# Masked attentions: value products of two query tiles together, key block by key block

## The chip, the cores and the metric

The kernel runs on one core of one Trainium2 chip. The metric is the device time of one execution in microseconds (us). PE is the matrix engine (TensorE; PEld its weight loads), ACT is ScalarE, DVE is VectorE, POOL is GpSimd, SP is SyncE, which issues most transfers.

## The reference, cut to what matters

The program is a chain of transformer layers over 512 tokens of width 1024: a convolution module, a feed-forward layer, a gate, a "forgetting" attention with 16 heads of 64, another feed-forward layer and gate, and a second block with three branches, one of them a block attention with 8 heads of 64. Both attentions with heads of 64 are causal and carry a bias per key:

```
s  = einsum("bqhd,bkhd->bhqk", q_blk, k) + bias      # q_blk: 128 queries
s  = where(k_pos <= q_pos, s, NEG_BIG)
pr = softmax(s, axis=-1)
o  = einsum("bhqk,bkhd->bqhd", pr, v)
```

In the second (`moba_attention`) a query sees its own block of 256 keys and up to three earlier ones. With 512 tokens there is one earlier block, which is always selected, so it too is causal attention over all keys, with a distance bias per head. Everything is in fp32.

## The kernel before, in words

Data lie with features on the partitions and the 512 tokens along the free axis. The large matrix products are done in three passes of a faster 32-bit format (high x high, high x low, low x high; L592 to L594), with weights that come from memory through `raw` and are split by ACT (L1062) and POOL (L485). Most of the time goes into these. The attentions are between them: the first between the projections of keys and values and the output projection, the second between two branches of the second block.

`head_attention` is written once for each of PE, ACT and DVE, and called for both attentions (`fox`, 8 head pairs; `mob`, 4 head pairs), with the biases fetched by SP or made by POOL. Each engine runs its own list of instructions in the order written; semaphores tie them together. Work is cut into groups: group `i` is one head pair (`j = i // 4`, heads `hh` = 0 and 1) and one tile of 128 queries, in the order of `ROW_TILE = (0, 3, 1, 2)`. A causal tile `qb` sees `qb + 1` key blocks of 128, so that the groups of a pair have 1, 4, 2 and 3 blocks. `s = 2 * i + hh` numbers a group's heads. For a group:

- PE `S_`: scores, 64 rows deep, both heads side by side (L855), and the causal mask as a product with a triangle (L857).
- DVE `B_`: bias, minimum and row maximum (L1880), into the group's own buffer of `prob_of` (in T and U).
- ACT `E_`: exponential with the row sum (L1327).
- DVE `R_`: reciprocal (L1887) and weighting (L1891).
- PE `T_`: transpositions, one per head and key block, with the identity (L866), into bank 2 + `hh` of `ms`. It waits for the weighting, and for the copy that last emptied this bank (`pt_copied`).
- ACT `C_`: the copy of a head's turned weights to `probT` (L1335). There are four such buffers of 512 columns: `U[:, 1]`, `acc_sq` and the two halves of `sqb`; buffer `s % 4` is free when the value products two groups back are done (`pv_done`).
- PE `V_`: value products, per key block and head a product of 64 value columns with 128 turned weights, added up over key blocks in bank 2 + `j % 2` of `gp` (L877).
- After a pair's last group: ACT `H_` (L1339) copies the output's high half, DVE `L_` (in the helper at L1532) makes its low half.

The order on PE is set by hand: iteration `i` does `S_(i)`, `T_(i - 3)`, `V_(i - 4)`. On ACT it is, for each of the two heads, the copy `C_` of group `i - 3` and the exponential `E_` of group `i`, and in every fourth iteration `H_`. On DVE it is `B_` of group `i` and `R_` of group `i - 1`, and in every fourth iteration `L_`. Of an fp32 product the trace has two records for each matmul, except for transpositions, which have one.

`wgx` is a gate weight of a later branch; it is cleared by POOL and filled by transfers after the first attention, and last read before the second.

Of the kernel before, what the change touches and what calls it, by code (L numbers as in the profile page):

```python
# [18 lines left out]
F32 = mybir.dt.float32  # L19
# [3 lines left out]
ACT = mybir.ActivationFunctionType  # L23
AX = mybir.AxisListType

P = 128
S = 512
D = 1024
KB = D // P
QB = S // P  # L30
# [15 lines left out]
ROW_TILE = (0, 3, 1, 2)  # L46
# [66 lines left out]
def build(nc, hbm, out):  # L113
# [6 lines left out]
    def phase(slabs=0, blks=0, rows=8, src=0, tiles=4, wide=False, **more):  # L120

        at = {"slab": led.take("slab", slabs), "blk": led.take("blk", blks)}
        of = rows if isinstance(rows, list) else [-1 if wide else rows] * slabs
        slab_at.extend(src + s // 2 for s in range(0, slabs))
        b = at["blk"]
        for s, r in enumerate(of):  # L130
            if wide:
                b += 4 * (s % 4 == 2)
                freed_at.append(Wide(led.take("wide", s % 4) + 1) if s % 4 < 2 else b)
                continue
            b += 8 // r if r else tiles * (1 - s % 2)
            freed_at.append(b)
        rows_of.extend(of)
        at.update({k: led.take(k, n) for k, n in more.items()})
        return at
# [22 lines left out]
    gq = phase(slabs=8, blks=8, src=53)  # L162
    gk = phase(slabs=8, blks=8, src=57)
    gv = phase(slabs=8, blks=8, wide=True, src=61)
    fox = phase(split=8, step=64, weighted=64, pt=64, pv=32)
    wo = phase(slabs=8, src=65, blks=8, split=8, sq=8, acc=7, norm=1, stat=1)
    plan_ffn(1)
    fin = phase(split=8)
# [8 lines left out]
    gkm = phase(slabs=4, blks=4, src=120)  # L177
    gvm = phase(slabs=4, blks=4, wide=True, src=122)
    br[0] = phase(slabs=12, blks=16, rows=branch_rows, src=124, sg=8, gm=8)
    mob = phase(split=4, step=32, weighted=32, pt=32, pv=16)  # L180
    br[1] = phase(slabs=12, blks=16, rows=branch_rows, src=130, sg=8, gm=8)
    mrg = phase(split=8)
    wout = phase(slabs=8, src=136, blks=8, split=8, sq=8, acc=7, norm=1, stat=1)
# [4 lines left out]
    with ExitStack() as ctx:  # L188
        def sb(name, shape, dt=F32, where=ctx):
            return where.enter_context(nc.sbuf_tensor(name, shape, dt))  # L190
# [15 lines left out]
        inv_d = sb("inv_d", [P, P])  # L206
        ident, identb, tri = sb("ident", [P, P]), sb("identb", [P, P], BF16), sb("tri", [P, P], BF16)
        T = sb("T", [P, 4, S])
        U = sb("U", [P, 2, S])
        acc_sq, sqb = sb("acc_sq", [P, S]), sb("sqb", [P, 2, S])  # L210
        rstd, var = sb("rstd", [P, S]), sb("var", [P, S])
        mkv = sb("mkv", [P, 4 * S])
        mk = mkv[:, 0:4 * MEM].rearrange("p (c s) -> p c s", c=4)
# [22 lines left out]
        with ExitStack() as lc:  # L236
            merged = sb("merged", [P, KB, S], F32, lc)
            with ExitStack() as c1:
                qx = sb("qx", [P, 4, S], F32, c1)
            with ExitStack() as c2:  # L240
                xap = sb("xap", [P, 4, S + 3], F32, c2)
                ga = sb("ga", [P, 4, S], F32, c2)
                xc = sb("xc", [P, 4, S], F32, c2)
                wga, wgx = sb("wga", [P, 4, P], F32, c2), sb("wgx", [P, 4, P], F32, c2)
            with ExitStack() as c3:
                qm, vm = sb("qm", [P, 4, S], F32, c3), sb("vm", [P, QB, HALF], F32, c3)
                mbias = sb("mbias", [P, 4, S], F32, c3)
                dist = sb("dist", [P, S], F32, c3)
        with ExitStack() as ld:
# [2 lines left out]
        big = u_pad[:, :, TAPS - 1:]  # L252
        bigs, proj_sb = (big, big1), kT
        prob, probT = T, (U[:, 1, :], acc_sq, sqb[:, 0, :], sqb[:, 1, :])
        prob_of = (T[:, 2, 3 * P:], T[:, 3, 3 * P:], U[:, 0, 0:2 * P], U[:, 0, 2 * P:],
                   T[:, 2, 0:3 * P], T[:, 3, 0:3 * P], T[:, 0, :], T[:, 1, :])
        token_half = (slice(0, S // 2), slice(S // 2, S))
# [4 lines left out]
        mcol = sb("mcol", [P, 2])  # L262
        mem_sq = mkv[:, :].rearrange("p (k s) -> p k s", k=KB)
        SP_OPS = 9 + len(ATANH)
        def whole_at(i):

            return TAPS - POOL_TAPS[i] - PE_TAPS[i]
# [15 lines left out]
        def conv_end(i, s=1):  # L283
# [3 lines left out]
        gp = ctx.enter_context(nc.psum_tensor("gp", [P, 4, S], F32))  # L287
        ms = ctx.enter_context(nc.psum_tensor("ms", [P, 4, S], F32))
# [37 lines left out]
        scored, biased, exped, transposed, pt_copied, pv_done, sum_inv = (  # L326
            sem("scored"), sem("biased"), sem("exped"), sem("transposed"), sem("pt_copied"), sem("pv_done"),
            sem("sum_inv"))
# [7 lines left out]
        step_open, weighted = sem("step_open"), sem("weighted")  # L336
# [247 lines left out]
        def _(pe):  # L584
# [252 lines left out]
            def head_attention(at, n, queries, keys, values, before):  # L837

                t0, N = at["step"], 4 * n

                def S_(i):
                    j, qb = i // 4, ROW_TILE[i % 4]
                    w, bank = (qb + 1) * P, (ms, gp)[i % 2]
                    if i == 1:
                        for c in range(2):
                            wait_evac(pe, before, c)  # L850
                    if i >= 2:
                        pe.wait_ge(biased, t0 + 2 * i - 2)
                    for hh in range(2):
                        r = slice(64 * hh, 64 * hh + 64)
                        pe.matmul(bank[:, hh, 0:w], queries[r, j, qb * P:qb * P + P], keys[r, j, 0:w], start=True, stop=False)  # L855
                    for hh in range(2):
                        pe.matmul(bank[:, hh, qb * P:w], identb[:], tri[:], start=False, stop=True).then_inc(scored, 1)  # L857

                def T_(i):
                    for hh in range(2):  # L860
                        s = 2 * i + hh
                        pe.wait_ge(weighted, at["weighted"] + s + 1)
                        if i:
                            pe.wait_ge(pt_copied, at["pt"] + s - 1)
                        for kb in range(ROW_TILE[i % 4] + 1):
                            m = pe.transpose(ms[:, 2 + hh, kb * P:kb * P + P], prob_of[2 * ROW_TILE[i % 4] + hh][:, kb * P:kb * P + P], ident[:])  # L866
                        m.then_inc(transposed, 1)

                def V_(i):
                    j, qb = i // 4, ROW_TILE[i % 4]  # L870
                    pe.wait_ge(pt_copied, at["pt"] + 2 * i + 2)
                    if i % 4 == 0 and j >= 2:
                        pe.wait_ge(lo_done, at["split"] + j - 1)
                    for kb in range(qb + 1):
                        for hh in range(2):
                            c = j * P + 64 * hh
                            m = pe.matmul(gp[64 * hh:64 * hh + 64, 2 + j % 2, qb * P:qb * P + P], values[:, kb, c:c + 64],  # L877
                                          probT[(2 * i + hh) % 4][:, kb * P:kb * P + P], start=(kb == 0), stop=(kb == qb),
                                          skip_group_check=True)
                    m.then_inc(pv_done, 1)  # L880

                for i in range(N + 4):
                    if i < N:
                        S_(i)
                    if 3 <= i < N + 3:
                        T_(i - 3)
                    if i >= 4:
                        V_(i - 4)

            head_attention(fox, 8, qT, kT, v_s, Pos(gv["blk"] + 4))  # L890
            gemm(wo, A, ready=fox["split"])
# [155 lines left out]
        def _(act):  # L1047
# [46 lines left out]
            for s, ready in enumerate((half_ready, raw_ready[0])):  # L1094
                src, at = part(Pos(s))
# [224 lines left out]
            def head_attention(at, X, k0, n):  # L1320
                t0, N = at["step"], 4 * n

                def E_(s):
                    w = (ROW_TILE[s // 2 % 4] + 1) * P
                    act.wait_ge(biased, t0 + s + 1)
                    p = prob_of[2 * ROW_TILE[s // 2 % 4] + s % 2][:, 0:w]
                    act.activation(p, p, ACT.Exp, scale=-1.0, bias=nmax[:, s % 8:s % 8 + 1], accum_out=rsum[:, s % 8:s % 8 + 1]  # L1327
                                   ).then_inc(exped, 1)

                def C_(s):  # L1330
                    w = (ROW_TILE[s // 2 % 4] + 1) * P
                    act.wait_ge(transposed, t0 + s + 1)
                    if s >= 4:
                        act.wait_ge(pv_done, at["pv"] + s // 2 - 1)
                    act.activation(probT[s % 4][:, 0:w], ms[:, 2 + s % 2, 0:w], ACT.Copy).then_inc(pt_copied, 1)  # L1335

                def H_(j):
                    act.wait_ge(pv_done, at["pv"] + 4 * (j + 1))
                    act.activation(X[0][:, k0 + j], gp[:, 2 + j % 2], ACT.Copy).then_inc(hi_done, 1)  # L1339

                for i in range(N + 3):
                    for s in (2 * i, 2 * i + 1):
                        if i >= 3:
                            C_(s - 6)
                        if i < N:
                            E_(s)
                    if i >= 8 and i % 4 == 0:
                        H_(i // 4 - 2)
                H_(n - 1)
# [942 lines left out]
```

## Time and profile before

| | |
|---|---|
| median of 3 runs | 2135.89 us (2135.56 to 2137.75) |
| profiled execution | 2135.93 us, its span 2134.1 us |
| PE busy | 2090.2 us (98%), granted clock 0.995 of full |
| ACT, DVE busy | 800.4 us (38%), 1012.6 us (47%) |
| the first attention on PE | 769.9 to 846.5 us |
| the second attention on PE | 1577.7 to 1619.5 us |

A record's length on PE is a modelled latency, and matmuls overlap: their pace is the distance of their starts. In a timeline, equal neighbours are merged ("x16"): the first number is the start of the first, the second the time from there to the end of the last. What stands in brackets is the engine's idle time before it and the releaser that the view infers from semaphores.

### The profile page before, as it was taken

How to read it: one execution, taken by the hardware profiler on the slowest of the kernel's cores; microseconds unless marked ns; L12 is line 12 of the kernel's file. 1: busy time of each engine (PE TensorE's matmuls, PEld its weight loads, DVE VectorE, ACT ScalarE, POOL GpSimd, SP SyncE). 2: the span in 40 equal slices, each digit the busy share in tenths (PEclk: the TensorE clock that was granted, in tenths of full speed). 3: DMA queues.
4: the chain of work that ended last, by engine and by line, in shares of the span. 5: the costliest groups of instructions: out<-in, count | busy, mean ns of one | idle time of the engine just before them, and what ended most of it. 6: DMA issues, size and time to landing. Idle time of an engine off the chain costs nothing.

```text
span 2134.1 us, 26391 instructions
## 1 busy us (share of the span) xinstructions
PE 2090.2 (98%) x9842; PEld 1697.7 (80%) x9842; DVE 1012.6 (47%) x1584; ACT 800.4 (38%) x1235; POOL 937.9 (44%) x437
## 2 busy tenths in 40 slices
PE   8998999999999999999999999999999999999998
PEld 6776888888888866888888887878867888888887
DVE  7996623122364556442131355573454456254463
ACT  6755422222353157322222355352244343222222
POOL 5984544444444420354444442444442444444442
PEclk9998999999999999999999999999999999999999
DMA  5332322222222221232222221322211222222221
GB/s 192 117 131 79 138 99 99 98 98 98 99 80 100 99 90 63 88 118 99 98 98 98 98 81 60 104 79 99 99 60 60 91 91 97 106 90 99 98 98 60
DMA packets 34523, 205.31 MB, mean 96 GB/s; under 512 B 4592, under 2 KB 6768, under 8 KB 11520
## 3 DMA queue, kind: packets, MB, share of 16 engines
q1 hardware_dynamic: 34144, 199.87, 26.8%
q10 hardware_dynamic: 288, 4.19, 0.5%
q8 instruction: 60, 0.98, 0.2%
q14 instruction: 31, 0.25, 0.0%
HBM read 197.73 MB, written 6.32 MB: 96 GB/s over the span
## 4 chain that ended last, share of the span: by engine, by line
PE 59%; issue 23%; POOL 10%; DVE 6%; ACT 1%; DMA 0%; POOLq 0%; DVEq 0%; ACTq 0%
PE gp L592 18%; PE gp L594 18%; PE gp L593 18%; POOL w_lo L485 9%; DVE ms L1535 4%; POOL pool_sum L508 1%; PE gp L640 0%; PE gp L639 0%; PE gp L638 0%; PE ms L729 0%; PE gp L937 0%; PE gp L877 0%; DMA raw<-w_hbm 0%; PE ms L740 0%; DVE T L1532 0%
## 5 line engine op out<-in xcount | busy, mean ns | idle before, releaser
L485 POOL TENSOR_TENSOR w_lo<-raw,w_hi 128x1024 fp32r<-128x1024 f32 x350 | 848.5, 2427 | 1102.0 <-ACT w_hi L1062 1080.3
L592 PE MATMUL gp<-a_hi,w_hi 128*128 128x512 f32 (+1 forms) x1456 | 568.2, 390 | 9.7 <-DVE a_lo L1535 8.8
L594 PE MATMUL gp<-a_hi,w_lo 128*128 128x512 f32 (+1 forms) x1456 | 563.9, 387 | 0.0
L593 PE MATMUL gp<-a_lo,w_hi 128*128 128x512 f32 (+1 forms) x1456 | 563.8, 387 | 0.0
L1062 ACT ACTIVATE w_hi<-raw 128x1024 fp32r<-128x1024 f32 x349 | 365.6, 1051 | 507.9 <-PE gp L594 436.9
L593 PE MATMUL gp<-b_lo,w_hi 128*128 128x512 f32 (+1 forms) x1216 | 470.4, 387 | 0.0
L592 PE MATMUL gp<-b_hi,w_hi 128*128 128x512 f32 x1184 | 463.8, 392 | 3.3 <-DVE b_lo L1532 3.3
L594 PE MATMUL gp<-b_hi,w_lo 128*128 128x512 f32 x1184 | 461.4, 390 | 0.0
L592 PEld LDWEIGHTS gp<-a_hi,w_hi 128*128 128x128 f32 x1456 | 273.9, 188 | 68.4 <-issue 10.5
L593 PEld LDWEIGHTS gp<-a_lo,w_hi 128*128 128x128 f32 x1456 | 274.0, 188 | 57.0 <-issue 1.4
L594 PEld LDWEIGHTS gp<-a_hi,w_lo 128*128 128x128 f32 x1456 | 273.8, 188 | 55.6
L1532 DVE TENSOR_TENSOR h<-gp,h 128x512 f32<-128x512 f32 (+1 forms) x106 | 72.2, 681 | 424.4 <-PE gp L594 424.4
L593 PEld LDWEIGHTS gp<-b_lo,w_hi 128*128 128x128 f32 x1216 | 229.0, 188 | 47.5 <-issue 1.2
L592 PEld LDWEIGHTS gp<-b_hi,w_hi 128*128 128x128 f32 x1184 | 222.8, 188 | 52.3 <-issue 5.6
L594 PEld LDWEIGHTS gp<-b_hi,w_lo 128*128 128x128 f32 x1184 | 222.6, 188 | 46.2
L1532 DVE TENSOR_TENSOR T<-gp,rstd 128x512 f32<-128x512 f32 x136 | 93.8, 691 | 309.0 <-PE gp L594 306.8
L1535 DVE SCALAR_TENSOR_TENSOR ms<-u_pad,par,ms 128x512 f32<-128x512 f32 x176 | 120.2, 757 | 0.8
L1071 ACT ACTIVATE sqb<-h 128x512 f32<-128x512 f32 x61 | 38.4, 630 | 129.7 <-DVE h L1532 116.3
L1535 DVE SCALAR_TENSOR_TENSOR T<-gpad,par,T 128x512 f32<-128x512 f32 x48 | 83.4, 1737 | 5.2 <-DVE T L2114 0.2
L508 POOL TENSOR_TENSOR pool_sum<-pool_sum,sqb 128x512 f32<-128x512 f32 x48 | 61.1, 1292 | 11.0 <-ACT sqb L1153 11.0
L1253 ACT ACTIVATE b_hi<-U 128x512 fp32r<-128x512 f32 x32 | 20.3, 634 | 121.3 <-DVE U L1535 121.3
L1253 ACT ACTIVATE a_hi<-U 128x512 fp32r<-128x512 f32 x32 | 20.3, 634 | 120.6 <-DVE U L1535 120.6
(327 smaller groups left out, 1797.2 us busy)
## 6 DMA issues: line engine op xcount, KB each, us to landing
raw<-w_hbm SPq DMA_DIRECT2D x175, 1024.0 KB, 4.8
proj_scratch<-kT ACTq DMA_DIRECT2D x2, 2048.0 KB, 6.9
fbias<-negc_scratch SPq DMA_DIRECT2D x16, 256.0 KB, 3.4
h<-x_hbm SPq DMA_DIRECT2D x8, 256.0 KB, 7.6
u_pad<-proj_scratch SPq DMA_DIRECT2D x1, 2048.0 KB, 9.8
big<-proj_scratch SPq DMA_DIRECT2D x1, 2048.0 KB, 8.8
out_hbm<-h SPq DMA_DIRECT2D x8, 256.0 KB, 2.2
raw<-w_hbm SPq DMA_DIRECT2D x2, 512.0 KB, 6.6
```

The source lines that it names most:

```text
L485: g.tensor_tensor(at(w_lo), src, f32(at(w_hi)), ALU.subtract).then_inc(w_lo_done, 1)
L508: g.tensor_tensor(pool_sum[:, s], pool_sum[:, s], sqb[:, s], ALU.add).then_inc(pool_conv, 1)
L592: pe.matmul(o, wh, xh, start=start, stop=False)
L593: pe.matmul(o, wh, xl, start=False, stop=False)
L594: return pe.matmul(o, wl, xh, start=False, stop=stop)
L1062: act.activation(at(w_hi), src, ACT.Copy).then_inc(w_hi_done, 1)
L1071: act.activation(dst, h[:, c], ACT.Square).then_inc(sq_done, 1)
L1253: act.activation(H_[0][:, k], U[:, k % 2], ACT.Copy).then_inc(hi_done, 1)
L1532: return v.tensor_tensor(o, a, b, op)
L1535: return v.scalar_tensor_tensor(o, a, s, b, op0, op1)
```

## The change

The value products of two consecutive groups of a pair (a "couple" `m`, groups `2m` and `2m + 1`: query tiles 0 and 3, or 1 and 2) are done in one batch. For each key block and head there is one product: where both tiles see the block, with 256 columns, else with 128. A batch has four or three key blocks (8 or 6 products) and comes in odd iterations: after `T_(i - 3)` comes the batch with groups `i - 5` and `i - 4`; even iterations have none, and the last batch stands behind the loop.

So that the two tiles' turned weights for one key block are neighbours, the copies go to slots of 128 columns in a tensor `turned` of 20 slots: five for each head of a couple, and two couples. Tile 3 goes to four slots in a row and tile 0 to the one ahead of it; tile 1 goes to slots 1 and 3, and tile 2 to slots 0, 2 and 4, whose blocks are transposed in the order 2, 0, 1. A copy now waits until the batch of the couple two before is done. `U`, `acc_sq` and `sqb` become parts of one tensor `scratch` with six rows, five of which are `turned`; `wgx` moves into the sixth.

```diff
-    fox = phase(split=8, step=64, weighted=64, pt=64, pv=32)
+    fox = phase(split=8, step=64, weighted=64, pt=64, pv=16)
...
-        U = sb("U", [P, 2, S])
-        acc_sq, sqb = sb("acc_sq", [P, S]), sb("sqb", [P, 2, S])
+        scratch = sb("scratch", [P, 6, S])
+        U, acc_sq, sqb = scratch[:, 0:2], scratch[:, 2], scratch[:, 3:5]
...
+        turned = scratch[:, 1:6].rearrange("p r (n c) -> p (r n) c", c=P)
...
+        turn_order = ([0], [0, 1], [2, 0, 1], [0, 1, 2, 3])
+
+        def turned_keys(m, hh, kb):
+
+            a = 10 * (m % 2) + 5 * hh
+            n, tiles = ((0, 2), (2, 1), (3, 1), (4, 1))[kb] if m % 2 == 0 else ((1, 2), (3, 2), (0, 1))[kb], (0, 3) if m % 2 == 0 else (1, 2)
+            return turned[:, a + n[0]:a + n[0] + n[1]], tiles[2 - n[1]:]
+
+        def turned_tile(m, hh, qb):
+
+            a = 10 * (m % 2) + 5 * hh
+            return turned[:, a:a + 1] if qb == 0 else turned[:, a + 1:a + 5] if qb == 3 else turned[:, a + 1:a + 4:2] if qb == 1 else turned[:, a:a + 5:2]
...
-                        for kb in range(ROW_TILE[i % 4] + 1):
-                            m = pe.transpose(ms[:, 2 + hh, kb * P:kb * P + P], prob_of[2 * ROW_TILE[i % 4] + hh][:, kb * P:kb * P + P], ident[:])
+                        qb = ROW_TILE[i % 4]
+                        for n, kb in enumerate(turn_order[qb]):
+                            m = pe.transpose(ms[:, 2 + hh, n * P:n * P + P], prob_of[2 * qb + hh][:, kb * P:kb * P + P], ident[:])
                         m.then_inc(transposed, 1)
 
-                def V_(i):
-                    j, qb = i // 4, ROW_TILE[i % 4]
-                    pe.wait_ge(pt_copied, at["pt"] + 2 * i + 2)
-                    if i % 4 == 0 and j >= 2:
+                def V_(m):
+                    j = m // 2
+                    pe.wait_ge(pt_copied, at["pt"] + 4 * m + 4)
+                    if m % 2 == 0 and j >= 2:
                         pe.wait_ge(lo_done, at["split"] + j - 1)
-                    for kb in range(qb + 1):
+                    for kb in range(QB - m % 2):
                         for hh in range(2):
                             c = j * P + 64 * hh
-                            m = pe.matmul(gp[64 * hh:64 * hh + 64, 2 + j % 2, qb * P:qb * P + P], values[:, kb, c:c + 64],
-                                          probT[(2 * i + hh) % 4][:, kb * P:kb * P + P], start=(kb == 0), stop=(kb == qb),
-                                          skip_group_check=True)
-                    m.then_inc(pv_done, 1)
-
-                for i in range(N + 4):
+                            keys_of, tiles = turned_keys(m, hh, kb)
+                            o = gp[64 * hh:64 * hh + 64, 2 + j % 2].rearrange("p (t c) -> p t c", c=P)
+                            o = o[:, tiles[0]:tiles[0] + 1] if len(tiles) == 1 else o[:, tiles[0]:tiles[1] + 1:tiles[1] - tiles[0]]
+                            mm = pe.matmul(o, values[:, kb, c:c + 64], keys_of, start=(kb == 0), stop=(kb == QB - 1 - m % 2), skip_group_check=True)
+                    mm.then_inc(pv_done, 1)
+
+                for i in range(N + 3):
                     if i < N:
                         S_(i)
-                    if 3 <= i < N + 3:
+                    if i >= 3:
                         T_(i - 3)
-                    if i >= 4:
-                        V_(i - 4)
+                    if i >= 5 and i % 2:
+                        V_((i - 5) // 2)
+                V_(N // 2 - 1)
...
                 def C_(s):
-                    w = (ROW_TILE[s // 2 % 4] + 1) * P
+                    m, qb, hh = s // 4, ROW_TILE[s // 2 % 4], s % 2
                     act.wait_ge(transposed, t0 + s + 1)
-                    if s >= 4:
-                        act.wait_ge(pv_done, at["pv"] + s // 2 - 1)
-                    act.activation(probT[s % 4][:, 0:w], ms[:, 2 + s % 2, 0:w], ACT.Copy).then_inc(pt_copied, 1)
+                    if m >= 2:
+                        act.wait_ge(pv_done, at["pv"] + m - 1)
+                    act.activation(turned_tile(m, hh, qb), ms[:, 2 + hh, 0:(qb + 1) * P].rearrange("p (r c) -> p r c", c=P), ACT.Copy
+                                   ).then_inc(pt_copied, 1)
```

The high half's wait becomes `pv_done` at 2 per pair instead of 4, and the second attention's count of batches 8 instead of 16.

## Rows read from the trace of the kernel before

**Rows 1.** The page, part 1: busy time, share of the span, instructions
```profile
PE 2090.2 (98%) x9842; PEld 1697.7 (80%) x9842; DVE 1012.6 (47%) x1584; ACT 800.4 (38%) x1235; POOL 937.9 (44%) x437
```

**Rows 2.** Windows: stretch, us, busy us of PE, PEld, DVE, ACT, POOL, clock, DMA
```profile
770.00:846.00 76.00, 72.52 (x666) 45.27 (x668) 58.22 (x232) 63.77 (x200) 2.35 (x1) 1.00 0.13 43
1582.00:1620.00 38.00, 34.54 (x320) 21.80 (x317) 28.96 (x104) 29.56 (x94) 4.17 (x4) 1.00 0.01 2
...
784.90:794.15 9.25, 9.03 (x88) 5.70 (x84) 7.25 (x30) 7.88 (x26) 0.00 (x0) 1.00 0.17 59
...
821.88:831.12 9.24, 9.02 (x88) 5.70 (x84) 7.25 (x30) 7.88 (x26) 0.00 (x0) 1.00 0.18 60
```

**Rows 3.** Timeline of PE, one head pair: start us, us, what, count, [idle before]
```profile
812.73 0.49 PE L855 MATMUL ms<-kT,qT 64*128 64x128 f32 x4
...
813.28 1.04 PE L866 MATMUL ms<-ident,T 128*128 128x128 f32 x8
814.25 0.32 PE L877 MATMUL gp<-U,v_s 128*64 128x128 f32 x1
...
814.41 0.27 PE L877 MATMUL gp<-U,v_s 128*64 128x128 f32 x1
...
814.62 1.13 PE L855 MATMUL gp<-kT,qT 64*128 64x512 f32 x4
...
816.34 1.09 PE L877 MATMUL gp<-sqb,v_s 128*64 128x128 f32 x16
817.36 0.70 PE L855 MATMUL ms<-kT,qT 64*128 64x256 f32 x4
...
818.84 0.52 PE L866 MATMUL ms<-ident,T 128*128 128x128 f32 x3 [0.23 <-DVE T L1891]
819.29 0.32 PE L877 MATMUL gp<-U,v_s 128*64 128x128 f32 x1
...
819.88 0.92 PE L855 MATMUL gp<-kT,qT 64*128 64x384 f32 x4
...
820.85 0.39 PE L866 MATMUL ms<-ident,T 128*128 128x128 f32 x2
821.17 0.88 PE L877 MATMUL gp<-sqb,v_s 128*64 128x128 f32 x12
821.97 0.49 PE L855 MATMUL ms<-kT,qT 64*128 64x128 f32 x4
```

**Rows 4.** Timeline of ACT, the same head pair
```profile
813.92 0.60 ACT L1335 ACTIVATE sqb<-ms 128x512 f32<-128x512 f32 x1
...
815.66 0.59 ACT L1339 ACTIVATE a_hi<-gp 128x512 fp32r<-128x512 f32 x1
...
817.62 0.72 ACT L1327 ACTIVATE T<-T,nmax 128x512 f32<-128x512 f32 x1 [1.00 <-DVE nmax L1880]
...
818.34 0.36 ACT L1335 ACTIVATE acc_sq<-ms 128x256 f32<-128x256 f32 x1
...
820.17 0.48 ACT L1335 ACTIVATE sqb<-ms 128x384 f32<-128x384 f32 x1
```

**Rows 5.** Timeline of DVE, the same head pair
```profile
814.30 0.75 DVE L1891 TENSOR_SCALAR T<-T,rinv 128x384 f32<-128x384 f32 x2
816.28 0.69 DVE L1532 TENSOR_TENSOR a_lo<-gp,a_hi 128x512 fp32r<-128x512 f32 x1 [1.23 <-ACT a_hi L1339]
```

**Rows 6.** Timeline of PE in the ramp of the first attention
```profile
774.37 0.39 PE L866 MATMUL ms<-ident,T 128*128 128x128 f32 x2
774.69 0.49 PE L855 MATMUL ms<-kT,qT 64*128 64x128 f32 x4
```

**Rows 7.** Timeline of PE and of ACT at the end of it
```profile
845.72 0.88 PE L877 MATMUL gp<-sqb,v_s 128*64 128x128 f32 x12
...
844.79 0.87 ACT L1335 ACTIVATE sqb<-ms 128x384 f32<-128x384 f32 x2 [1.06 <-PE ms L866]
```

**Rows 8.** One line's instructions: ns min/median/max
```profile
L1062 ACT ACTIVATE w_hi<-raw x349: 1039/1046/1065, 24.4 to 2101.5; 128x1024 fp32r<-128x1024 f32 x175
```

More of the change, by code:

```diff
@@ L179, in build @@
     br[0] = phase(slabs=12, blks=16, rows=branch_rows, src=124, sg=8, gm=8)
-    mob = phase(split=4, step=32, weighted=32, pt=32, pv=16)
+    mob = phase(split=4, step=32, weighted=32, pt=32, pv=8)
     br[1] = phase(slabs=12, blks=16, rows=branch_rows, src=130, sg=8, gm=8)
@@ L243, in build @@
                 xc = sb("xc", [P, 4, S], F32, c2)
-                wga, wgx = sb("wga", [P, 4, P], F32, c2), sb("wgx", [P, 4, P], F32, c2)
+                wga, wgx = sb("wga", [P, 4, P], F32, c2), scratch[:, 5].rearrange("p (j c) -> p j c", c=P)
             with ExitStack() as c3:
@@ L1330, in C_ @@
                 def C_(s):
-                    w = (ROW_TILE[s // 2 % 4] + 1) * P
+                    m, qb, hh = s // 4, ROW_TILE[s // 2 % 4], s % 2
                     act.wait_ge(transposed, t0 + s + 1)
-                    if s >= 4:
-                        act.wait_ge(pv_done, at["pv"] + s // 2 - 1)
-                    act.activation(probT[s % 4][:, 0:w], ms[:, 2 + s % 2, 0:w], ACT.Copy).then_inc(pt_copied, 1)
+                    if m >= 2:
+                        act.wait_ge(pv_done, at["pv"] + m - 1)
+                    act.activation(turned_tile(m, hh, qb), ms[:, 2 + hh, 0:(qb + 1) * P].rearrange("p (r c) -> p r c", c=P), ACT.Copy
+                                   ).then_inc(pt_copied, 1)
                 def H_(j):
-                    act.wait_ge(pv_done, at["pv"] + 4 * (j + 1))
+                    act.wait_ge(pv_done, at["pv"] + 2 * (j + 1))
                     act.activation(X[0][:, k0 + j], gp[:, 2 + j % 2], ACT.Copy).then_inc(hi_done, 1)
```

## The prediction

> **What bounds the kernel now.** The page comes first: the matrix engine is busy 2090.2 of 2134.1 us, and no other engine passes 48% [rows 1]. Such a share is of intervals that overlap, so I went on to the windows of the two masked attentions. There the matrix engine is still the fullest (72.5 of 76 us and 34.5 of 38 us, clock at full speed), but ScalarE is busy 84% and VectorE 77% of the first attention, where over the whole program it is 38% and 47%; one pair of heads takes 9.24 us, five times running (the first and the last are shown), of which ScalarE is busy 7.88 [rows 2]. So here the question is not "how much does the matrix engine do" but "who waits for whom", and that is read from the three engines' timelines of one head pair, 812.7 to 822.0.
>
> On the matrix engine every iteration is scores (L855), mask (L857), turning (L866), value products (L877) [rows 3]. The two heads' value products start together, on 64 columns each; a pair of records of 128 columns follows the last after 0.109 us: 16 records take (1.09-0.27)/7.5. That is 128 columns at two cycles of 2.4 GHz (0.107) and 0.002 over. Entering and leaving a batch costs more: the last transposition before 814.25 starts at 813.28+1.04-0.27=814.05, so 0.20 passes where 0.11 is the pace; the second pair follows the first after 0.16 instead of 0.11; and at the exit 0.20 passes again.
>
> There is one stall in the pair: three transpositions start at 818.84 after idling [rows 3]. The view names the weighting on VectorE, but that group's weighting was over at 814.30+0.75=815.05 [rows 5]; the instruction also waits until the bank it writes has been copied out, and that copy ran 818.34 to 818.70 on ScalarE [rows 4], 0.14 before 818.84. The copy was late because ScalarE executes in order: it stood behind the exponential of 817.62, which had idled 1.00 for VectorE's biased scores, which stood behind the low half of the previous pair's output (816.28, idle 1.23), which waited for ScalarE's high half of 815.66 [rows 4, 5]. That half comes back to back behind the copy of 813.92. This closes a ring, and the ring gives the period: copy of 813.92 to the end of the copy at 818.70, 4.78; wake-up 0.14; 818.84 to the value products at 819.29, 0.45; these to the scores at 819.88, 0.59; to 820.85, 0.97; to 821.17, 0.32; to 821.97, 0.80; scores to the next such copy (812.73 to 813.92), 1.19. Sum 9.24, the measured period [rows 2 to 4].
>
> **The change, part by part.** *Matmuls.* A head pair has 20 value products (2 heads x 10 key blocks); they become 14, since blocks shared by two query tiles run once at 256 columns. Columns stay. Streaming costs the same 0.107 per pass and block; six pair slots fewer at 0.002 each are 0.01 us.
>
> *Batches.* Four become two per pair, each of five blocks. The batch of one block (814.25 to 814.62, 0.37) and that of two (0.59) go, and their blocks come back in the next iteration's batch at 0.21 each: 0.37-0.21 and 0.59-0.43, 0.16 twice. The scores now follow a transposition directly; that succession stands in the ramp: transpositions at 774.37 (two, last start 774.48) and scores at 774.69, 0.20 again [rows 6], so the exit price stays and the entry price alone goes. Gross gain on the matrix engine 0.33 per pair, 3.9 us over 12 pairs. If nothing but the matrix engine counted, that would be the answer.
>
> The Trainium skill says two things of this place. Its page "TensorE: Matmul & The Clock Gate" (section on what happens when a matmul is issued) says that weight loads are pulled ahead of running matmuls; by it, entering a batch would be free, the gross gain only 0.01 x 12=0.1, and the first rival below 2135.8 instead of 2132.0. "TensorEngine Tiling (Array Packing)", Key Properties, says "Mode switching requires drain"; by it going from 128x128 to 128x64 costs, and the gain of 3.9 stands. The rows at 814.25 side with the second [rows 3].
>
> *The copies' wait.* ScalarE's copy waited for the value batch two groups back; now it waits for the batch two pairs of groups back, which is issued at least two iterations before the transposition. It did not wait before and doesn't now: nothing.
>
> *The copies' pattern.* For two and three blocks the destination is now in pieces of 128 elements that begin 256 apart; the source stays contiguous. No row has a scattered destination on ScalarE. Nearest: the weight copies of L1062, most of which read eight pieces of 128 and some one piece of 1024; all lie within 1039 to 1065 ns [rows 8]. I take 0; above, 0.02 per copy (the spread of these), and since three such copies lie in the ring (818.34, 820.17 and the one between them), 0.06 x 12=0.7 us; below, nothing, as the number of elements stays.
>
> *The order.* This decides. In iterations with an even number there is no value batch now; in odd ones it has five blocks. Take the pair above. Up to the copy ending at 818.70 the ring is ScalarE and VectorE alone, and scores come earlier, not later: 818.84 stays where it is. From 819.29 the scores go first: they would be done 0.59 early, and the next transpositions could start at 820.26 and 820.37. But the second of them writes the bank whose copy runs 820.17 to 820.65 [rows 4], back to back behind exponentials since 817.62, so it can't be moved by the matrix engine. Before, it met a bank just free (820.85 plus 0.11); now it waits until 820.65+0.14=820.79. And behind it stands the whole batch: 0.20 to enter, then five blocks. Four blocks take 817.36-816.34=1.02; one more is 0.22, merging gives back 0.01: 1.23. The scores come at 822.22, where they came at 821.97. The new ring: ScalarE 813.92 to 820.65, 6.73; 0.14; 0.20; 1.23; 1.19; sum 9.49, **0.25 longer** per pair. The two blocks that used to fill the copy's shadow have moved behind it. The wait of 818.84 grows too (the matrix engine arrives 0.15 earlier), which costs nothing.
>
> *Ramp and tail.* The first pair runs before the ring has closed; it can gain between nothing and 0.33, and as its second head's transposition already waits for a copy I take 0.10. At the end, the last batch but one stands ahead of the last transpositions and has five blocks instead of four (+0.21); the last one starts only when the last copies are done (844.79+0.87=845.66, batch at 845.72 [rows 7]), and the two blocks that ran in their shadow come behind (+0.43): +0.64. The output's high and low halves and the next phase's first matmuls follow as before.
>
> *Memory.* Four scratch rows become one tensor with a fifth row, lent by a gate weight that is cleared and used between the attentions; no instruction is added, no queue passed. Nothing.
>
> **The sum.** First attention, eight pairs: -0.10, five closed periods x 0.25, +0.64: 1.8. Second, four pairs, taken at the same durations since its busy shares are the same to a few per cent [rows 2]: -0.10, one period 0.25, +0.64: 0.8. Together +2.6 us. The profiled execution took 2135.93 (span 2134.1 and 1.8 around it), the median of the runs shown is 2135.89: the same. Forecast 2138.5 us, slower by 0.12%, which a measurement of this kernel (about 0.2%, 4.3 us) hardly tells from no change.
>
> **Rivals.**
> *The matrix engine's gain arrives.* If the second transposition does not meet a busy bank, 0.33 x 12=3.9 us come off: 2132.0. For it: the matrix engine is the fullest in every window, and ScalarE idles 1.00 in each pair. Against: the idle time lies inside the ring, not after it. It needs ScalarE's chain of 817.62 to 820.65 to begin some 0.4 earlier, for which nothing in the change provides.
> *The existing stall goes as well.* If moving work out of the even iterations lets the high half, the low half and with them 817.62 come earlier, up to the present wait at 818.84 goes: the idle 0.23 shown there counts from the modelled end of a record 0.27 long where the pace is 0.11, so the engine stood 0.23+0.16=0.39; x 12=4.7 more: 2127.3. Against: 815.66 is followed back to 813.92 with ScalarE never idle.
> *Slower than can be overlooked.* ScalarE's copies with a scattered destination cost more. The three on the ring each lengthen every period; at 0.08 each 0.24 x 12=2.9 us come on top, +5.5: 2141.4. It decides from 0.05 per copy (+4.4). For it: no row excludes it; ScalarE has no slack there. Against: [rows 8], for the source side.
> *The heads no longer run side by side.* If 256-column products of the two heads ran one after another, each batch would take 1.07 more, 24 x 1.07=26 us: 2164. For it: nothing; the scores run side by side up to 512 columns (1.13 for four records of 0.43).
>
> **Chances.** Forecast 0.62 (+1.0 to +4.2); full gain 0.16, half of it perhaps just past the bound; stall gone too 0.05; scattered copies 0.15; heads apart 0.02. Range 2132.5 to 2141.5: it takes in the unpriced copies above and most of the first rival below. Faster by over 0.2%: 0.13; within: 0.67; slower: 0.20.
>
> **What would show it.** In the timeline of a steady pair: no L877 between L866 and L855 in even iterations; batches of 8 and 6 pair slots, 1.2 us from first start to the scores; the single transposition's second head starting about 0.5 after the first, 0.14 behind the end of a 384-column copy; a period of 9.49; copies of 256 and 384 columns at 0.36 to 0.40 and 0.48 as now. L877 has 336 records for 480. The prediction is wrong if the period is 9.24 or less, if that transposition doesn't wait, or if the copies' durations moved.

## The result, and the profile after

The changed kernel takes **2140.62 us** (median of 13 runs, 2138.67 to 2141.48) against 2136.11 (13 runs): the ratio is 1.0019, 95% interval 1.0012 to 1.0026, so 2.6 to 5.6 us slower. The forecast was 2138.5 in a range of 2132.5 to 2141.5. It also said that a measurement would hardly tell the change from none; this interval does tell it. The profiled execution took 2141.31 with a span of 2138.5.

First the page, part 1, to be read against [rows 1]. The matrix engine (PE) has 144 records fewer (12 pairs x 12), and its busy share says nothing of the loss:

```profile
PE 2091.0 (98%) x9698; PEld 1695.6 (79%) x9698; DVE 1013.3 (47%) x1584; ACT 798.1 (37%) x1235; POOL 937.9 (44%) x437
```

Then two windows, each one head pair of the first attention, as in [rows 2]. A pair takes 9.52 us where it took 9.24, and every engine but VectorE is busy for less of it:

```profile
796.13:805.65 9.52, 8.89 (x76) 5.36 (x72) 7.36 (x30) 7.64 (x26) 0.00 (x0) 1.00 0.17 56
815.18:824.70 9.52, 8.89 (x76) 5.37 (x72) 7.36 (x30) 7.64 (x26) 0.00 (x0) 1.00 0.16 55
```

The timeline of PE for the second of these pairs answers to [rows 3]; L869 are scores, L881 transpositions, L895 value products:

```profile
815.26 0.49 PE L869 MATMUL ms<-kT,qT 64*128 64x128 f32 x4
...
815.80 1.04 PE L881 MATMUL ms<-ident,T 128*128 128x128 f32 x8
816.78 1.13 PE L869 MATMUL gp<-kT,qT 64*128 64x512 f32 x4
...
818.50 1.31 PE L895 MATMUL gp<-scratch,v_s 128*64 128x256 f32 x16
819.74 0.70 PE L869 MATMUL ms<-kT,qT 64*128 64x256 f32 x4
...
821.37 0.52 PE L881 MATMUL ms<-ident,T 128*128 128x128 f32 x3 [0.38 <-DVE T L1909]
821.82 0.92 PE L869 MATMUL gp<-kT,qT 64*128 64x384 f32 x4
...
822.79 0.28 PE L881 MATMUL ms<-ident,T 128*128 128x128 f32 x1
823.32 0.30 PE L881 MATMUL ms<-ident,T 128*128 128x128 f32 x1 [0.25 <-ACT scratch L1352]
823.55 1.30 PE L895 MATMUL gp<-scratch,v_s 128*64 128x256 f32 x12
824.78 0.49 PE L869 MATMUL ms<-kT,qT 64*128 64x128 f32 x4
```

The reader is to see the new stall: the single transposition of the second head starts 0.53 after the first (822.79, 823.32). It was 0.11 before, two records running together at 820.85 [rows 3]. Behind it stands the whole batch of five blocks. The timeline of ScalarE (ACT), against [rows 4], has what it waits for:

```profile
816.45 0.60 ACT L1352 ACTIVATE scratch<-ms 128x512 f32<-128x512 f32 x1 [0.79 <-PE ms L881]
...
820.14 0.72 ACT L1344 ACTIVATE T<-T,nmax 128x512 f32<-128x512 f32 x1 [1.09 <-DVE nmax L1898]
...
820.86 0.36 ACT L1352 ACTIVATE scratch<-ms 128x256 f32<-128x256 f32 x1
...
822.69 0.48 ACT L1352 ACTIVATE scratch<-ms 128x384 f32<-128x384 f32 x1
```

The ring of the forecast can be read off step by step: copy of 816.45 to the end of the copy at 823.17, 6.72; wake-up 0.15; transposition to batch 0.23; batch to scores 1.23; scores (815.26) to the next such copy (816.45) 1.19. Sum 9.52. ScalarE now idles 0.79 ahead of the first of these copies, which it did not before: it waits for a matrix engine that waits for it. The copies last 0.36 and 0.48 as before.

**Where the 5.4 us between the two profiled executions are.** The first scores of the first attention start at 769.90 before and 771.67 after: +1.77 before the change has done anything. The first attention, from there to the first matmul of the next stage, takes 76.62 and 78.40 (+1.78); the second 41.77 and 42.13 (+0.36). What is left of the span is +0.5, and outside the span are 1.83 and 2.81 (+1.0).

### The profile page after: what moved, and what is told of

It is laid out like the page before. It is cut to its first block, busy times and chain, and to the rows that moved or that the text cites. A ratio compares the mean times of both kernels' runs of the same rounds, so it can differ in the third digit from the quotient of the medians.

```text
span 2138.5 us, 26095 instructions
## 1 busy us (share of the span) xinstructions
PE 2091.0 (98%) x9698; PEld 1695.6 (79%) x9698; DVE 1013.3 (47%) x1584; ACT 798.1 (37%) x1235; POOL 937.9 (44%) x437
## 4 chain that ended last, share of the span: by engine, by line
PE 58%; issue 23%; POOL 10%; DVE 6%; ACT 2%; DMA 0%; POOLq 0%; SPq 0%; DVEq 0%; ACTq 0%
PE gp L606 18%; PE gp L608 18%; PE gp L607 18%; POOL w_lo L499 9%; DVE ms L1553 4%; POOL pool_sum L522 1%; DMA raw<-w_hbm 0%; PE gp L895 0%; PE ms L743 0%; PE gp L654 0%; PE gp L652 0%; PE gp L653 0%; PE gp L954 0%; PE ms L754 0%; DVE T L1550 0%
## 5 line engine op out<-in xcount | busy, mean ns | idle before, releaser
L1088 ACT ACTIVATE scratch<-h 128x512 f32<-128x512 f32 x70 | 44.1, 630 | 159.9 <-DVE h L1550 136.8
L522 POOL TENSOR_TENSOR pool_sum<-pool_sum,scratch 128x512 f32<-128x512 f32 x48 | 61.3, 1294 | 12.9 <-ACT scratch L1170 12.8
L1270 ACT ACTIVATE b_hi<-scratch 128x512 fp32r<-128x512 f32 x32 | 20.3, 634 | 121.3 <-DVE scratch L1553 121.3
L1270 ACT ACTIVATE a_hi<-scratch 128x512 fp32r<-128x512 f32 x32 | 20.3, 634 | 120.6 <-DVE scratch L1553 120.6
```

The lines of the kernel that those rows point to most:

```text
L522: g.tensor_tensor(pool_sum[:, s], pool_sum[:, s], sqb[:, s], ALU.add).then_inc(pool_conv, 1)
L1088: act.activation(dst, h[:, c], ACT.Square).then_inc(sq_done, 1)
L1270: act.activation(H_[0][:, k], U[:, k % 2], ACT.Copy).then_inc(hi_done, 1)
```

## The experiments

In each of them two theories stood against each other; in most the leading one was the ring of the prediction, in the rest (layout, repetition, biases) it was about the start-up or GpSimd. All ratios are to runs of the kernel before on the same chip in the same session.

### The layout alone

```diff
-        U = sb("U", [P, 2, S])
-        acc_sq, sqb = sb("acc_sq", [P, S]), sb("sqb", [P, 2, S])
+        scratch = sb("scratch", [P, 6, S])
+        U, acc_sq, sqb = scratch[:, 0:2], scratch[:, 2], scratch[:, 3:5]
...
-                wga, wgx = sb("wga", [P, 4, P], F32, c2), sb("wgx", [P, 4, P], F32, c2)
+                wga, wgx = sb("wga", [P, 4, P], F32, c2), scratch[:, 5].rearrange("p (j c) -> p j c", c=P)
```

> The kernel before with one edit: U, acc_sq and sqb are parts of one tensor with a sixth row, and the gate weight wgx lies in that row. No instruction changes. The trace of the changed kernel starts its first attention at 771.7 us instead of 769.9, with the same instructions ahead of it, and this is what is tested. Theory (the ring alone makes the change slower; the 1.8 us ahead of it are the chance of where half-clock stretches of the first 200 us fall): 2136.1 +- 0.7, head pairs 9.24 us apart, first scores at 769.9 in some executions and later in others, whatever the layout. Rival (moving the scratch rows shifts every later tensor and costs time in the convolution stage): first scores at 771.7 and 2137.9, every time.

Measured: 2136.3, ratio 1.000 (0.9991 to 1.0009); first scores at 769.47, pairs 9.24 to 9.25 apart, attentions 76.63 and 41.78 long. The layout costs nothing.

### Layout, slots and copies, but the old batches

```diff
-                            keys_of, tiles = turned_keys(m, hh, kb)
...
+                            a = 10 * (i // 2 % 2) + 5 * hh
+                            a += (0, 1 + 2 * kb, (2, 4, 0, 0)[kb], 1 + kb)[qb]
+                            m = pe.matmul(gp[64 * hh:64 * hh + 64, 2 + j % 2, qb * P:qb * P + P], values[:, kb, c:c + 64],
+                                          turned[:, a], start=(kb == 0), stop=(kb == qb), skip_group_check=True)
```

> The changed kernel with the old order of the value products: four batches per head pair, one per group, 128 columns each, 20 products; what is kept is the layout, the order of the transpositions and the copies into scattered slots. Theory (the order of the batches closes the longer ring): head pairs 9.24 us apart as before, 2136.1 plus what the start-up varies (up to 1.8). Rival (ScalarE's copies with a scattered destination cost more and lengthen the ring): copies of 256 and 384 columns longer than 0.36 to 0.40 and 0.48, head pairs 9.24 + 3 x the excess apart.

Measured: 2136.36, ratio 0.9999 (0.9990 to 1.0008); pairs 9.24 apart. The timeline of ScalarE of this kernel has the scattered copies (256 and 384 columns), as long as the contiguous ones in [rows 4]:

```profile
818.17 0.36 ACT L1351 ACTIVATE scratch<-ms 128x256 f32<-128x256 f32 x1
...
820.00 0.48 ACT L1351 ACTIVATE scratch<-ms 128x384 f32<-128x384 f32 x1
```

So the rival of the scattered copies falls, and the loss in the attentions comes from the batches.

### The same batches, not merged

```diff
-                            mm = pe.matmul(o, values[:, kb, c:c + 64], keys_of, start=(kb == 0), stop=(kb == QB - 1 - m % 2), skip_group_check=True)
...
+                        for n, tile in enumerate(tiles):
+                            for hh in range(2):
...
+                                mm = pe.matmul(gp[64 * hh:64 * hh + 64, 2 + j % 2, tile * P:tile * P + P], values[:, kb, c:c + 64],
+                                               keys_of[:, n], start=(kb == 0), stop=(kb == tile), skip_group_check=True)
```

> The changed kernel with the same batches, two per head pair in odd iterations, but each key block's products one per query tile again: 20 products of 128 columns instead of 14. Theory (the merging is worth 0.002 us per pair slot, 0.01 per head pair, and the place of the batches is all that counts): head pairs 9.53 us apart, as the changed kernel's 9.52, and the same time within 0.5. Rival (weight loads matter, six of twenty saved): head pairs 0.05 to 0.3 further apart than in the changed kernel, over 12 pairs 0.6 to 3.6 us.

Measured: pairs 9.53 apart, attentions 78.49 and 42.17 long (changed kernel 78.40 and 42.13). This kernel begins the sums of two tiles in turn in one bank, and its output is wrong; it serves for times alone, as every product, copy and wait is there. The merging is worth 0.01 per pair in the attention; the batches' place is what costs. Its whole time was 2139.23, ratio 1.0013 (1.0004 to 1.0022).

### The low half one iteration later, in the kernel before

```diff
-                    if i >= 8 and i % 4 == 0:
+                    if i >= 9 and i % 4 == 1:
                         L_(i // 4 - 2)
+                L_(n - 2)
                 L_(n - 1)
```

> The kernel before with one edit: VectorE makes the low half of a pair's output one iteration later, behind the biased scores it now holds up. The ring of 9.24 us runs through this low half (0.61 of it). Theory: the ring opens, the stall of 0.39 us per pair in the matrix engine goes, and the matrix engine's own sum of 9.24 - 0.39 = 8.85 is what is left (8.75 to 8.85); over 9 closed periods and the ramps that is -3.5 us: 2132.6. Rival (the stall is due to the weighting on VectorE, which the view names): VectorE's order gives the weighting no earlier start, the stall stays and the head pairs stay 9.24 apart, 2136.1.

Measured: 2133.05, ratio 0.9985 (0.9976 to 0.9993). Pairs are 8.83 apart. In PE's timeline the two heads' three-block transpositions (818.12 and 818.84 in the kernel before, with the stall between) are one run of six, and scores follow at the period of 8.83:

```profile
811.49 0.49 PE L855 MATMUL ms<-kT,qT 64*128 64x128 f32 x4
...
816.88 0.82 PE L866 MATMUL ms<-ident,T 128*128 128x128 f32 x6
...
820.32 0.49 PE L855 MATMUL ms<-kT,qT 64*128 64x128 f32 x4
```

The weighting, which the view names as the releaser of that stall, stands ahead of the low half in VectorE's list in both kernels and was not moved. The stall was the copy's, and the copy's delay was the low half's.

### The low half one iteration later, in the changed kernel

The same edit.

> The changed kernel with the same edit: the low half one iteration later. Theory (the change saves 0.33 us per pair on the matrix engine, and only the ring turned this into a loss): with the ring open the head pairs are 8.55 to 8.65 apart, below those of the kernel before with the same edit by 0.1 to 0.3, and the time is 2132.0 plus what the start-up varies (up to 1.8); against the changed kernel as it is about -7. Rival (the five-block batches are bad by themselves, since the second head's transposition in the odd iteration waits for its copy whatever VectorE does): head pairs stay above 9.24 apart.

Measured: 2133.74, ratio 0.9985 (0.9976 to 0.9994). Pairs are 8.73 apart instead of 9.52, 0.10 below the kernel before with the same edit; attentions 73.66 and 40.46 long against 74.13 and 40.47. The change has turned from a loss of 2.1 us in the attentions into a gain of 0.5. The whole times do not show this gain (2133.74 and 2133.05, the same ratio of 0.9985). The forecast had 8.55 to 8.65: it missed, because a shorter stall of the same kind is left. In PE's timeline of the changed kernel with both edits (below), where nothing holds the second, the two one-block transpositions look like this:

```profile
816.28 0.39 PE L881 MATMUL ms<-ident,T 128*128 128x128 f32 x2
```

In PE's timeline of this kernel, with the low half moved alone, they take 0.22 more:

```profile
817.70 0.61 PE L881 MATMUL ms<-ident,T 128*128 128x128 f32 x2
```

### Copies ahead of exponentials, in the kernel before

```diff
                     for s in (2 * i, 2 * i + 1):
                         if i >= 3:
                             C_(s - 6)
+                    for s in (2 * i, 2 * i + 1):
                         if i < N:
                             E_(s)
```

> The kernel before with one edit on ScalarE: in each iteration both heads' copies stand ahead of both heads' exponentials (copy, copy, exponential, exponential instead of copy, exponential, copy, exponential); the low half stays where it was. Theory (the copy is late only because it stands behind an exponential that waits for VectorE): the stall at the second head's transposition goes, head pairs 8.83 us apart as with the later low half, and the tail and the second attention gain as well: 2131.0 (-5). Rival (the low half itself on VectorE is what the matrix engine waits for, through the scores' bias): the biased scores come as late as before, and the head pairs stay above 9.0 apart.

Measured: 2129.28, ratio 0.9965 (0.9952 to 0.9979), or 7.9 us below the 2137.13 of that session, where the forecast had 5. Pairs are 8.83 apart although the low half still stands ahead of the biased scores, and the ramps gain too: attentions 73.05 and 38.52 long. The low half matters only by what queues behind it on ScalarE.

### Copies ahead of exponentials, in the changed kernel

The same edit.

> The changed kernel with copies ahead of exponentials on ScalarE, the low half where it was. The ring of the forecast ran through the copy of the group with two query blocks into that with three; with the copies first, the last copy still stands behind the two exponentials of 0.72 and 0.71 that wait for the low half. Theory: one stall of about 0.3 stays per pair in the batch of five blocks, head pairs 8.75 to 8.85 apart, the same as the kernel before with this edit (8.83), so that the change is worth nothing there: attention about 73.0 long, total 2130.5. Rival (copies first opens everything): 8.51, as with both edits.

Measured: 2131.22, ratio 0.9976 (0.9966 to 0.9986). Pairs are 8.76 apart, attentions 73.15 and 39.15 long, against 73.05 and 38.52: with this edit alone the change is a loss of 0.7 again, though the pairs are 0.07 closer. The closer pairs give 0.35 in the first attention, but the tail is 0.37 longer in each (15.09 us from the last pair's first scores to the next stage, against 14.72), and the second attention has only one closed period to set against it. In PE's timeline of this kernel the stall sits where it was expected, with 0.25 at the one-block transpositions (0.64 against 0.39):

```profile
816.95 0.64 PE L881 MATMUL ms<-ident,T 128*128 128x128 f32 x2
```

### Both edits in the changed kernel

> The changed kernel with both edits: copies ahead of exponentials on ScalarE, and the low half one iteration later. Theory: nothing but the matrix engine is left in the period, so that the change's gross gain arrives in full: 8.83 - 0.33 = 8.50 us between head pairs, first attention 71 to 72 us long (before 76.6, changed 78.4), about 2129.5 (-7) plus what the start-up varies. Rival (ScalarE, busy 7.9 of each period, becomes the bound itself): head pairs stay at 8.73, as with the low half alone.

Measured: 2128.45, ratio 0.9962 (0.9949 to 0.9976): the lowest median of all. In PE's timeline nothing waits any more; five blocks follow the transpositions at once:

```profile
809.32 0.49 PE L869 MATMUL ms<-kT,qT 64*128 64x128 f32 x4
...
814.78 0.60 PE L881 MATMUL ms<-ident,T 128*128 128x128 f32 x4
815.31 0.92 PE L869 MATMUL gp<-kT,qT 64*128 64x384 f32 x4
...
816.60 1.30 PE L895 MATMUL gp<-scratch,v_s 128*64 128x256 f32 x12
817.83 0.49 PE L869 MATMUL ms<-kT,qT 64*128 64x128 f32 x4
```

Pairs are 8.51 apart (809.32 to 817.83), 0.32 below the 8.83 of the old batches with the ring open. That is the gross gain of 0.33 that the prediction read from the trace of before. The attentions are 71.56 and 38.25 long, 1.8 us less together than with the old batches and copies first (73.05 and 38.52). Over the whole kernel the two, run in turn, are 2128.45 and 2129.28; their spans (medians) 2125.7 and 2127.4. The intervals of their ratios overlap (five runs each), so the whole time alone does not separate them. The kernel before with both edits was not run: its pairs could not come below 8.83, where its matrix engine already waits for nothing, but its second attention (10.00 and 8.51 between pairs here, 9.84 and 8.98 there) might gain from the later low half. ScalarE is not the bound at 8.51.

### The changed kernel once more

> The changed kernel once more, unchanged, for its start. In its profile the first scores came at 771.7 us, in those of the kernel before and of the two variants with the new layout at 769.5 to 769.9. Theory (half-clock stretches of the matrix engine in the first 200 us fall differently from one execution to the next): this time 769.5 to 771.7, with the attention 78.4 long whatever the start; the median is 2140.0 +- 1. Rival (the changed program starts late by itself): 771.7 again, 2140.6.

Measured: 2139.5, ratio 1.0016 (1.0007 to 1.0025); in its profile the first scores are at 769.74, and the attentions 78.38 and 42.13 long. So the late start of the first profile is no property of the program. The kernel before with the copies first had it as well (first scores at 771.36). What differs, the windows of that profile show (stretch and its us; the granted clock is the third number from the end):

```profile
24.00:30.00 6.00, 5.33 (x15) 3.94 (x16) 3.59 (x7) 4.83 (x7) 2.71 (x2) 0.72 0.13 25
136.00:144.00 8.00, 6.61 (x13) 3.02 (x14) 8.00 (x14) 3.47 (x7) 5.34 (x4) 0.79 0.40 131
182.00:202.00 20.00, 14.99 (x50) 11.68 (x50) 11.30 (x21) 16.77 (x25) 6.07 (x4) 0.57 0.18 66
```

The same windows in the second profile of the same kernel:

```profile
24.00:30.00 6.00, 5.58 (x23) 4.30 (x24) 3.57 (x6) 4.83 (x6) 2.98 (x2) 1.00 0.21 45
136.00:144.00 8.00, 7.26 (x23) 4.31 (x24) 8.00 (x14) 2.85 (x7) 4.88 (x3) 1.00 0.38 131
182.00:202.00 20.00, 14.98 (x56) 11.54 (x57) 11.32 (x20) 17.22 (x25) 5.44 (x3) 0.66 0.15 52
```

The stages are the same; in the first profile the matrix engine had its lower level (1.2 of 2.4 GHz) for part of the first two stretches, in the second it had the full one. In the third the level was low for part of the stretch in both, longer in the first. In each, the engine is not busy throughout. Elsewhere it is the other way round (94 to 100: 1.00 in the first, 0.72 in the second). Over 20 to 210 the granted clock is 0.94 and 0.96; from these, an estimate of what the difference can cost is up to 0.02 x 190, some 4 us. That is enough for the 1.9 between the two starts, but no run takes the clock apart from all else.

### The biases of the second attention, left out

```diff
-                    g.tensor_tensor(mbias[:, r % 4], dist[:], col("slope", r).broadcast_to([P, S]), ALU.mult).then_inc(mb_ready, 1)
+                    w = S if j < 2 else 4
+                    g.tensor_tensor(mbias[:, r % 4, 0:w], dist[:, 0:w], col("slope", r).broadcast_to([P, w]), ALU.mult).then_inc(mb_ready, 1)
```

> The kernel before with GpSimd computing only 4 of the 512 columns of the distance bias for the head pairs 2 and 3 of the second attention (this part of the computation is left out; the waits stay). In the second attention two weightings on VectorE take 1.16 and 1.13 us instead of 0.35 while GpSimd makes these biases, twice. Theory (the two engines hold each other up there, and that is why the second attention's pairs lie further apart than the first's): pairs 10.3 and 9.24 us apart as in the first attention (now 11.12 and 10.37), attention 39.8 us long (now 41.8). Rival (something else of the second attention, as its narrower loads from another tensor): 11.1 and 10.4 again.

> The changed kernel with the same part left out. Theory (the second attention lost only 0.4 and not the forecast 0.8 because the collision with GpSimd covers part of the longer ring): pairs 10.24 and 9.52 apart (now 11.39 and 10.00), attention 40.5 long, 0.65 to 0.7 longer than the kernel before with the same part left out. Rival (the second attention gains where the first loses): the difference stays at 0.4.

Measured, by one profile each: kernel before, pairs 10.32 and 9.24 apart, attention 39.84 long; changed kernel 10.24 and 9.52, attention 40.51 long. The difference is 0.67, and both kernels now have the first attention's distances. (With the biases whole, they are 11.12 and 10.37 in the kernel before, 11.39 and 10.00 in the changed one.) In the timeline of VectorE, changed kernel with its biases whole (start, duration, instructions):

```profile
1588.33 2.20 DVE L1909 TENSOR_SCALAR scratch<-scratch,rinv 128x256 f32<-128x256 f32 x2
```

In the timeline of GpSimd, same kernel and place:

```profile
1588.29 2.08 POOL L571 TENSOR_TENSOR mbias<-dist,par 128x512 f32<-128x512 f32 x2 [8.52 <-DVE nmax L1898]
```

And the same two weightings in VectorE's timeline of the changed kernel with the biases cut, where GpSimd is quiet:

```profile
1586.66 0.62 DVE L1910 TENSOR_SCALAR scratch<-scratch,rinv 128x256 f32<-128x256 f32 x2
```

## Why the prediction was right, and where its sizes were off

- **The bound.** That the attentions are held by a ring through ScalarE and VectorE, and not by the matrix engine that is busy 95% of them, is shown: taking the low half out of it or moving the copies ahead of the exponentials brings the pairs from 9.24 to 8.83, near the 8.85 that the ring's stall of 0.39 left.
- **The gross gain** of 0.33 per pair is shown at 0.32 (8.83 to 8.51), once the ring is open for both. Of the two readings that the prediction weighed, this bears out the one by which entering a batch costs something (by the other the gain would have been 0.01). By what mechanism entering costs, no run separates.
- **The rival at 3.9 us.** This gain times 12 was too much all the same: with nothing waiting, the two attentions became 1.8 us shorter, since it comes in full only in closed periods (five in the first attention, 1.6 us); the first pairs and the tails gave none of it (9.41 and 9.47 between the second and third pair, 14.72 and 14.75 in the tail).
- **The longer ring**: forecast 9.49, measured 9.52. The 0.03 is the step from the held transposition to the batch, 0.23 instead of 0.20.
- **Nothing for slots, copies, layout**: shown by two kernels at 1.000. That the two heads still run side by side at 256 columns shows in the batch, 1.23 as forecast.
- **A slip in a working.** The pace of 0.109 was got by dividing 0.82 by 7.5. Sixteen records are eight pairs and so seven steps, of which the first is 0.16: (0.82-0.16)/6 is 0.11, so the pace stands.
- **Ramp and tail of the first attention**: forecast -0.10 and +0.64. Measured in starts: the first pair -0.08; from the last pair's first scores to the next stage 15.30 before, 15.77 after, +0.47. The last transpositions come only 0.04 later after those scores than before (13.03, 12.99). The forecast had +0.21 there, for the longer batch ahead of them, and overlooked two things: the last pair too carries the longer ring up to its next transpositions (9.24 before, 9.53 after: +0.29), and behind these the batch of one block and its waits are gone (2.72 before, 2.26 after: -0.46). The +0.43 of the two blocks behind the last copies came in full. The whole first attention came to +1.78 for 1.8, since the period's excess (5 x 0.28) made up for the smaller tail: two misses of about 0.15 that happened to offset each other.
- **The second attention**: forecast +0.8, measured +0.36. This is the term that was mis-sized. The forecast took the first attention's durations "since its busy shares are the same to a few per cent"; yet its pairs are 11.12 and 10.37 apart, not 10.32 and 9.24, because GpSimd's biases hold up two weightings, twice. There the change makes the first of these two distances longer by 0.27 and the second shorter by 0.37. With the biases left out the difference is 0.67: the first attention's durations (-0.08, +0.28, +0.47).
- **The rest.** Attentions +2.1, forecast +2.6; the whole kernel +4.1 by the ratio, and +3.4 by the second one (+4.5 and +2.4 by the medians). So about half of the loss of the first measurement has no term in the forecast, and that this part stayed small enough for the range is luck, as nothing in the prediction bounded it. Of the rest, 0.4 in the first profile of the changed kernel and 0.5 in the second lie in the last microseconds. There the last four matmuls (L1030 before, L1047 after) ran at full clock in the profile of before, and all or most of the time at the lower level in both profiles of the changed kernel (granted clock 0.50 and, in the first, 0.55). PE's timeline before:

```profile
2127.63 1.10 PE L1030 MATMUL gp<-T,inv_d 128*128 128x256 f32 x4 [1.21 <-ACT T L1513]
```

PE's timeline in the second profile of the changed kernel:

```profile
2129.66 2.04 PE L1047 MATMUL gp<-T,inv_d 128*128 128x256 f32 x4 [1.21 <-ACT T L1531]
```

  The forecast took everything after the attentions as shifted; it had no term for where the clock falls. This is not tied to the merged batches either: with the later low half the same four matmuls take 2.04 in the kernel before (granted clock 0.50) and 1.10 in the changed kernel (1.00). A further 0.8 lies outside the span: run by run, 1.8 (median) in the kernel before and in the layout's, 2.0 with the old batches in slots or the batches not merged, 2.6 to 2.7 in the changed kernel and in its variants with the later low half, but 2.0 again in the changed kernel with the copies first alone. Within the changed kernel's own runs it goes from 2.0 to 3.2. **What this is stays open**; no view shows anything outside the span, and no run separates it. It is also why the fastest kernel gains less in time (0.8 on the old batches with copies first) than in span (1.7).

## What to carry to other kernels

When an engine is busy 95% of a stage, add up the steps around one period before taking its work away: if the sum runs through another engine's in-order queue, the work that is removed comes back as a wait, and the work moved behind that wait makes the period longer. A releaser that a view names is to be checked by its end: if it was done long before, look for the other semaphores that the instruction waits for. In such a ring, first move what queues ahead of the late instruction: here one reordering on ScalarE took 6.8 us off the attentions. Then look again before adding the change to the matrix engine. With the later low half alone it gained 0.5 in the attentions, with the copies first alone it lost 0.7, and each left one wait per pair at the second transposition; only with both, when nothing waited, did it gain 1.8.

## What had not been expected

- Two weightings of 256 columns on VectorE take 2.20 us instead of 0.62 while GpSimd makes two biases of 512 columns (2.08); the two engines end within 0.2 of each other. VectorE alone pays: GpSimd's four earlier biases, with VectorE idle, take 1.04 us each, and these two 1.04 and 1.09. It costs the second attention 1.9 us in the kernel before (41.77 to 39.84). The Trainium skill, "SBUF — State Buffer" (Who interferes with whom), has a tensor_scalar of VectorE in a "2-port perf mode" and GpSimd take one shared pair of ports by an exclusive lock, so that the later one "fully blocks". The trace agrees in what happens, 2.20 against 0.62; that the port is the cause no run here shows.
- The start of the first attention varies by 1.9 us (769.74 and 771.67) between executions of one program, along with the clock's low stretches in the first 200 us, as much as the smaller effects of this case; a difference of two profiles is to be split at fixed points of the program before it is explained.
